# A planned order for the attention stage, its output kept turned, and a mixing stage that loads rows turned

## The reference, cut to what matters

```
z = rms(x, g_pre_mix) @ w_in -> q, k, v, forget logits, B, C, u
s = q.k / 8 + c[query] - c[key], c = cumsum(log_sigmoid(f)), key <= query, 8 heads of 64
o_attn = softmax(s) @ v                     (the sample rows: 512 cached keys and their own 64)
o_conv = B * causal_conv3(C * u)            (512 channels)
merged = concat(rms(o_attn, g_attn_out), rms(o_conv, g_conv_out))
x = x + rms(merged @ w_o, g_post_mix)
x = x + rms(relu(rms(x, g_pre_mlp) @ w_up)^2 @ w_down, g_post_mlp)
```

## Time and profile before

| | us |
|---|---|
| median of three runs | 2732.44 |
| the profiled execution | 2737.44 |
| its span, first to last instruction | 2735.8 |
| PE busy | 2664.9 (97%) |
| DVE busy | 1515.6 (55%) |
| ACT busy | 1126.6 (41%) |
| POOL busy | 1300.7 (48%) |

### The profile page before, as it was taken

The page is one execution under the profiler, slowest core; times in us unless marked ns, Lnnn a source line. Parts: engine busy times, 40 slices in busy tenths (PEclk is TensorE's granted clock), DMA queues, the critical chain, the costliest instruction groups (busy, mean ns, idle before and its releaser), DMA issues.

```text
span 2735.8 us, 41595 instructions
## 1 busy us (share of the span) xinstructions
PE 2664.9 (97%) x14966; PEld 2405.3 (88%) x14966; DVE 1515.6 (55%) x2603; ACT 1126.6 (41%) x2099; POOL 1300.7 (48%) x884
## 2 busy tenths in 40 slices
PE   8999999998999999999999999899999999999997
PEld 8999999897888888888889989889999988999996
DVE  5233344247888887765344344665556564556554
ACT  3201301107777877555333332534333344333433
POOL 3233334220101006553477776766556677566654
PEclk9999999999999999999999999999999999999999
DMA  6643534574565443568444546421211272212213
GB/s 199 199 123 110 175 108 142 189 199 103 124 150 122 100 102 117 167 183 244 143 168 163 196 169 225 170 74 64 77 61 61 85 277 96 73 61 66 72 61 108
DMA packets 294353, 364.26 MB, mean 133 GB/s; under 512 B 37576, under 2 KB 245392, under 8 KB 290128
## 3 DMA queue, kind: packets, MB, share of 16 engines
q1 hardware_dynamic: 257152, 316.15, 37.7%
q0 software_dynamic: 11808, 26.74, 3.1%
q10 hardware_dynamic: 25264, 19.66, 2.1%
HBM read 264.30 MB, written 97.94 MB: 132 GB/s over the span
## 4 chain that ended last, share of the span: by engine, by line
PE 46%; DVE 2%; POOL 1%; DMA 1%; issue 1%; ACT 0%; SPq 0%; DVEq 0%; POOLq 0%; ACTq 0%
PE dn_bank L3006 17%; PE up_bank L2982 15%; PE dn_bank L2962 7%; PE up_bank L2937 7%; DMA m_raw_up<-in_w_up 1%; DVE m_raw_up L2758 1%; POOL m_y L2517 1%; POOL m_w_up L2466 1%; DVE m_t L2758 0%; SPq L2342 0%; ACT m_junk L2659 0%; DVE m_y L2863 0%; DMA m_x<-scratch_x 0%; POOL m_u L2509 0%; DVE m_y L2817 0%
## 5 line engine op out<-in xcount | busy, mean ns | idle before, releaser
L3006 PE MATMUL dn_bank<-m_w_dn,m_u 128*128 128x512 f32 x2304 | 531.0, 391 | 5.4 <-ACT m_y L2692 4.3
L3006 PEld LDWEIGHTS dn_bank<-m_w_dn,m_u 128*128 128x128 f32 x2304 | 432.7, 188 | 96.0 <-ACT m_y L2692 4.0
L2982 PE MATMUL up_bank<-m_h,m_w_up 128*128 128x384 f32 x2688 | 476.1, 337 | 8.7 <-DVE m_stage L2772 4.5
L2982 PEld LDWEIGHTS up_bank<-m_h,m_w_up 128*128 128x128 f32 x2688 | 470.1, 189 | 12.7 <-issue 5.1
L2819 DVE TENSOR_TENSOR m_y<-dn_bank,m_y 128x1024 f32<-128x1024 f32 x168 | 205.7, 1224 | 270.4 <-PE dn_bank L3006 270.4
L508 POOL TENSOR_TENSOR w_lo<-w_raw,w_hi 128x1024 fp32r<-128x1024 f32 x72 | 176.0, 2448 | 342.3 <-DVE w_hi L722 342.3
L2509 POOL TENSOR_TENSOR m_u<-m_stage,m_u 128x384 fp32r<-128x384 f32 x128 | 141.5, 1128 | 281.7 <-ACT m_u L2648 281.7
L2466 POOL TENSOR_TENSOR m_w_up<-m_raw_up,m_w_up 128x512 fp32r<-128x512 f32 x128 | 192.2, 1521 | 65.2 <-ACT m_w_up L2616 65.2
L938 PE MATMUL proj<-ha_hi,w_hi 128*128 128x384 f32 (+1 forms) x640 | 212.1, 331 | 0.0
L1446 DVE TENSOR_TENSOR p_lo<-t_bank,p_hi 128x512 fp32r<-128x512 f32 (+1 forms) x336 | 197.9, 599 | 25.2 <-ACT p_hi L1393 24.6
L938 PE MATMUL proj<-ha_hi,w_lo 128*128 128x384 f32 (+1 forms) x640 | 210.0, 328 | 0.0
(11 more groups left out here) (304 smaller groups left out, 5674.4 us busy)
## 6 DMA issues: line engine op xcount, KB each, us to landing
m_raw_up<-in_w_up SPq DMA_DIRECT2D x48, 1024.0 KB, 5.4
m_raw_dn<-in_w_down SPq DMA_DIRECT2D x47, 1024.0 KB, 4.9
w_raw<-in_w_in SPq DMA_DIRECT2D x72, 512.0 KB, 4.1
scratch_h_pairs<-m_pieces POOLq DMA_DIRECT2D x12, 1792.0 KB, 8.2
m_h<-scratch_h_pairs SPq DMA_DIRECT2D x14, 1536.0 KB, 10.8
nck<-scratch_ncum SPq DMA_DIRECT2D x8, 1312.0 KB, 19.2
scratch_v_hl<-vhl SPq DMA_DIRECT2D x20, 512.0 KB, 2.7
q_hi<-scratch_q_hi SPq DMA_DIRECT2D x16, 528.0 KB, 7.3
```

The costliest lines, as they stand in the source:

```text
L2982: mm = pe.matmul(out, w_up[:, j, wp, k, :], hidden_rows(g, j, hp, k), start=(k == 0 and p == 0), stop=(k == KH - 1 and p == 2))
L3006: mm = pe.matmul(bank[:, cols], part, wd[:, wp, b, cols], start=(b == 0 and p == 0), stop=(b == 1 and p == len(passes) - 1))
```

## The change

**The order.** `attention_order` is written anew: it simulates TensorE, VectorE and ScalarE with a cost for each step and lets each engine take, among the next S, M, T, V and O, the one that can start first (with a fixed preference where several can). The group EXTRA stands behind group 0. There are four s_banks instead of three, and no n_bank.

**The output stays turned.** ScalarE copies the two halves of the o_bank to partitions 0 to 63 (two copies of 64 partitions), GpSimd adds and scales them. The factors lie along columns now, so VectorE's reciprocals are stored to a scratch and loaded back, broadcast to 64 partitions. The result is stored to scratch_attn_t. The next head's loads are spread over the first three groups: queries and keys, decays, values.

**Mixing loads both kinds of rows turned.** No multiplication by g_attn or g_conv per tile: the gains are multiplied into w_o before it is split, one more GpSimd operation per block. GpSimd squares both kinds of rows, sums their blocks and forms both rests; TensorE makes two one-column products per tile and no turns of ag.

The diff, cut to its core (A_BUFS is the number of output buffers; the parts left out rename, drop what is no longer used, or move an operation as told above):

```diff
-S_BANKS, T_BANKS, O_BANKS = 3, 3, 1
-V_BEHIND = 3
-SPLITS = {(1, QT // 4): (4,), (1, 0): (5, 6), (1, 1): (7, 0, 1), (1, 2): (2, 3)}
+S_BANKS, T_BANKS, O_BANKS = 4, 3, 1
 P_BUFS = 4
-A_BUFS = 5
-DELAY = {"act": {"M": 6, "T": 1, "O": 3, "N": 2}, "dve": {"M": 1, "T": 3}}
+A_BUFS = 2
+GROUP_ORDER = (0, EXTRA, 1, 2, 3)
+SPLITS = {0: (5, 6), EXTRA: (4,), 1: (7, 0, 1), 2: (2, 3)}
+FIRST_CHOICE = {"pe": "TVS", "dve": "TS", "act": "OTM"}
...
+    def cost(engine, x):
+        if engine == "pe":
+            if x.kind == "S":
+                return 2 * (x.width / 2.4 + 13) + (107 if x.last else 0), 320
...
+            def store_scales(q):
+                line = dr["rtotal"][q.head:q.head + 1, q.rows]
+                sp.wait_ge(recip_done, q.k + 1)
...
+                    sp.dma_start(line.rearrange("o (a p) -> (o p) a", p=P), rtotal[:, sums(q)], allow_slow_non_contiguous=True).then_inc(rtotal_stored, 16)
+            def load_scales(q):
+                sp.wait_ge(rtotal_stored, 16 * (q.k + 1))
+                if q.k >= 2:
+                    sp.wait_ge(att_done, q.k - 1)
...
+                sp.dma_start(scales[0:HD, q.k % 2, 0:wide(q)], line.to_broadcast([HD, wide(q)])).then_inc(scales_loaded[q.k % 2], 16)
+            def fetch(head, at):
+                par = head % 2
+                if head >= 2 and at == 0:
+                    sp.wait_ge(used, P_BUFS + groups[GROUPS_OF * (head - 1) - 1].products[-1].at + 1)
+                if head == HEADS:
+                    if at == 0:
+                        front.load_weights(sp)
+                elif at == 0:
...
+            for q in groups:
+                fetch(q.head + 1, q.k % GROUPS_OF)
+                store_scales(q)
+                load_scales(q)
...
+                if q.k:
+                    store(groups[q.k - 1])
...
+            def close(q):
...
+                pool.wait_ge(o_taken, O_BANKS + q.k + 1)
...
+                pool.tensor_tensor(place, halves[0], halves[1], ALU.add).then_inc(added, 1)
+                pool.wait_ge(added, q.k + 1)
+                pool.wait_ge(scales_loaded[q.k % 2], 16 * (q.k // 2 + 1))
+                pool.tensor_tensor(place, place, scales[0:HD, q.k % 2, 0:wide(q)], ALU.mult).then_inc(att_done, 1)
+            for q in groups:
+                if q is final[3]:
+                    pool.wait_ge(taken, S_BANKS + ALL_TAKEN)
+                    front.set_ones(pool)
+                    front.sum_blocks(pool, 0, 0)
+                    front.rests(pool, 0, 0)
+                close(q)
+                if q.head == HEADS - 1 and q.g in SPLITS:
+                    for k in SPLITS[q.g]:
+                        front.split_weights(pool, k)
...
+                    act.wait_ge(used, P_BUFS + q.products[-1].at + 1)
+                    if q.k >= 2:
+                        act.wait_ge(added, q.k - 1)
+                    bank = o_bank[q.k % O_BANKS]
+                    act.activation(o_t[0:HD, q.k % 2, 0, 0:q.wide], bank[0:HD, 0:q.wide], ACT.Copy)
+                    act.activation(o_t[0:HD, q.k % 2, 1, 0:q.wide], bank[HD:P, 0:q.wide], ACT.Copy).then_inc(o_taken, 1)
...
     def split_weights(self, pool, k):
         pool.wait_ge(self.w_loaded[k], 16)
+        pool.wait_ge(self.S["gains_loaded"], 32)
+        pool.tensor_scalar(self.w_raw[:, k, :], self.w_raw[:, k, :], self.gains[:, k:k + 1], None, ALU.mult).then_inc(self.S["w_scaled"], 1)
...
+    def sum_blocks(self, pool, t, s):
...
+            pool.tensor_tensor(q[:, n], rows[:, s], rows[:, s], ALU.mult).then_inc(S["squared"], 1)
...
+        pool.tensor_tensor(q[:, :, 0:2, :], q[:, :, 0:2, :], q[:, :, 2:4, :], ALU.add).then_inc(S["halves_summed"], 1)
...
+        pool.tensor_tensor(self.square_sums[:, :, :], q[:, :, 0, :], q[:, :, 1, :], ALU.add).then_inc(S["blocks_summed"], 1)
+    def rests(self, pool, t, s):
...
+        pool.tensor_tensor(self.a_lo[:, s], self.a_in[:, s], self.a_hi[:, s].bitcast(F32), ALU.subtract).then_inc(S["a_lo_done"], 1)
...
+        pool.tensor_tensor(self.c_lo[:, s], self.c_in[:, s], self.c_hi[:, s].bitcast(F32), ALU.subtract).then_inc(S["c_lo_done"], 1)
...
-            last_rows["scores_free"]()
-            turn(0, 0)
+            last_rows["scores_free"](pe)
             pe.wait_ge(S["w_lo_done"], CJ)
             pe.wait_ge(S["c_lo_done"], 1)
             multiply(c_bank, c_hi, c_lo, 0, CJ, S["c_mult"], (0,))
```

More of the change, by code:

```diff
@@ new lines, with __init__ @@
+EXTRA = QT // 4
+GROUP_ORDER = (0, EXTRA, 1, 2, 3)
+SPLITS = {0: (5, 6), EXTRA: (4,), 1: (7, 0, 1), 2: (2, 3)}
+FIRST_CHOICE = {"pe": "TVS", "dve": "TS", "act": "OTM"}
+class Group:
+    def __init__(self, k, head, g):
+        self.k, self.head, self.g, self.par = k, head, g, head % 2
+        self.extra = g == EXTRA
+        self.tiles = [QT] if self.extra else list(range(4 * g, 4 * g + 4))
+        self.n = len(self.tiles)
+        self.rows = slice(SEQ, ROWS) if self.extra else slice(4 * g * P, 4 * g * P + 4 * P)
+        self.wide = P if self.extra else 512
+        self.set = 0 if self.extra else g % 2
+        self.before = None
+        self.scores, self.maxima, self.turns, self.products, self.out = [], [], [], [], None
@@ new lines, in __init__, with attention_steps, step @@
+        self.blocks, self.cols, self.turn = blocks, cols, turn
+        self.first, self.last = first, last
+        self.maximum, self.last_score = None, None
+def attention_steps():
+    groups, count = [], dict.fromkeys("SMTVO", 0)
+    def step(kind, group, **more):
+        count[kind] += 1
+        return Step(kind, group, count[kind] - 1, **more)
+    for head in range(HEADS):
+        for g in GROUP_ORDER:
+            q = Group(len(groups), head, g)
+            same = [p for p in groups if p.set == q.set and not (q.extra and p.head == head)]
+            q.before = same[-1] if same else None
+            for tile in q.tiles:
+                if q.extra:
+                    pieces = [(0, PAST), (PAST, DEC)]
+                else:
+                    pieces = [(c, min(512, (tile + 1) * P - c)) for c in range(0, (tile + 1) * P, 512)]
+                for n, (col, width) in enumerate(pieces):
+                    q.scores.append(step("S", q, tile=tile, n=n, col=col, width=width, last=n == len(pieces) - 1))
+                q.maxima.append(step("M", q, tile=tile, n=len(pieces), width=pieces[-1][0] + pieces[-1][1]))
+                for x in q.scores[-len(pieces):]:
+                    x.maximum = q.maxima[-1]
+                q.maxima[-1].last_score = q.scores[-1]
+            if q.extra:
+                units = [(tuple(range(CB)), slice(0, CB * P)), ((CB,), slice(0, P))]
+            else:
+                units = [((j,), slice(max(0, j - 4 * g) * P, 512)) for j in range(4 * g + 4)]
+            for n, (blocks, cols) in enumerate(units):
+                edge = dict(first=n == 0, last=n == len(units) - 1)
+                t = step("T", q, blocks=blocks, cols=cols, width=cols.stop - cols.start, **edge)
+                q.turns.append(t)
+                q.products.append(step("V", q, blocks=blocks, cols=cols, width=cols.stop - cols.start, turn=t, **edge))
+            q.out = step("O", q, width=q.wide)
+            groups.append(q)
+    return groups
@@ L1335, in _ @@
+            front.load_rows(sp)
+            store(groups[-1])
+            for q in groups[-A_BUFS:]:
+                stored(q)
         @block.gpsimd
         def _(pool):
-            pool.sem_inc(added, 1)
             pool.memset(q_hi[1][:, ROWS:].bitcast(F32), 0.0)
@@ L1406, in _ @@
[L1406 to L1415 removed]
+                    act.wait_ge(turned, 1 + x.at + 1)
+                    act.wait_ge(used, x.at + 1)
@@ L1417, in _ @@
+            for x in queues["act"]:
+                step(x)
         @block.vector
@@ L1502, in step @@
                     mm.then_inc(used, 1)
-                elif x.kind == "N" and not (x is last_n and it == AGAIN):
-                    pe.wait_ge(o_taken, O_BANKS + upto("N", it, x.at) + 1)
-                    pe.wait_ge(n_taken, upto("N", it, x.at) + 1)
-                    for i in range(4 if x.g < EXTRA else 1):
-                        mm = pe.transpose(n_bank[:, i * P:(i + 1) * P], o_t[:, x.at % 2, i * P:(i + 1) * P], ident[:, :])
-                    mm.then_inc(in_rows, 1)
-            loop(pe, "pe", step)
```

657 lines of the change are left out of this document (245 added, 412 removed).

## The result

| | us |
|---|---|
| changed kernel, median of four runs | 2905.42 (2899.59 to 2909.27) |
| kernel before, beside it, median of four | 2731.84 |
| ratio | 1.063, 95% interval 1.0609 to 1.0652 |
| forecast | 2713, range 2698 to 2731 |

The account below looks back on a forecast made before the run. TensorE's stream plus hand-over waits was taken to bound attention, the stream alone mixing. From 2737.44: -31 heads, +13.5 late mixing start, +1.7 clock, -3.7 mixing gave 2718; less 5.0 to the median, 2713 us, range 2698 to 2731.

Parts of the forecast that it names:

- I cost it at nothing in heads 0 to 6: Attention: the reciprocals' store and broadcast load add nothing in the first seven heads, being covered by 10 us.
- (c): Attention: factor round trips on SP pace the heads, deciding from about 5 us a store; 2776 at 7 us; chance 0.08.
- The MLP stage's code is the same; I put nothing there: MLP stage, behind mixing: no change in time, 0 us in the sum.
- I take the cast's 1.04: Last head, GpSimd: each of eight multiplications of w_o by the gains takes 1.04 us.
- W: Last head: issue of the w_o loads, 1028.80 in the kernel before; TensorE forecast to start mixing at W + 69.2.
- Heads: Attention, heads 0 to 6: 57.5 us falls to 53.1, gaining 4.4 each, 31 in all (13 to 40).
- (b): Attention: the new order moves waits instead of removing them, only the turns go; 2731 us, no change; chance 0.12.
- The last head: GpSimd's chain starts mixing 13.5 us later, TensorE idles 17 us, and a lower clock costs 1.7.
- the bound of 2.4: Last head, GpSimd: multiplication by the gains as slow as a two-input operation, 2.4 instead of 1.12 for each of eight, +10.
- (a): Start of mixing is not late: the reciprocals' store overtakes the loads or GpSimd has room; 2703 us; chance 0.14.
- Mixing: Mixing stage: TensorE loses the turns of ag and gains pairs of one-column sums, a gain of 3.7 us.
- (d): Mixing: GpSimd's operations are stretched and bound it, 13.4 us a tile instead of 12.3, +19, 2732 us; chance 0.04.

Follow-up runs that it names:

- e15: Changed kernel with the gains in dead bytes so that no tile is shifted, factor stores as they are: 2865.19 us, ratio 1.0480.
- e13: e1 with the gains in dead bytes so that no tile is shifted, outputs still not divided: 2716.52 us, ratio 0.9941.
- e1: Changed kernel with no reciprocals stored or loaded, scales filled once with 1.0, outputs not divided: 2734.65 us, ratio 1.0002.
- e12: Kernel before with 32 unused bytes added, shifting the tiles that the change shifted: 2758.37 us, ratio 1.0097.
- e14: Changed kernel with factors stored in 16-byte pieces and no tile shifted, gains' multiplications still on GpSimd: 2727.09 us, ratio 0.9979.
- e9: Changed kernel with 16-byte factor pieces, stored and loaded ahead of the next loads, gains multiplied on ScalarE, no tile shifted: 2704.77 us, ratio 0.9879.
- e6: Changed kernel with each stored factor 64 bytes from the next and scales loaded from another tensor, outputs wrongly scaled: 2743.55 us, ratio 1.0040.
- e2: Changed kernel with each 512-factor store writing 16-byte pieces, order in memory changed, outputs wrongly scaled: 2743.42 us, ratio 1.0034.
- e3: Changed kernel with each factor store issued twice, the second into its own scratch, both waited for: 2902.19 us, ratio 1.0622.
- e5: e1 with the gains' tile padded, so later tiles are shifted by 64 bytes instead of 32: 2742.31 us, ratio 1.0035.
- e8: Changed kernel with 16-byte factor pieces, stored and loaded ahead of the next loads, gains multiplied on ScalarE, gains' tile padded: 2729.09 us, ratio 0.9984.

## Why the prediction was wrong

**The step that failed** is "I cost it at nothing in heads 0 to 6". Its cover was worked out from when the factors come, with round trips of the size of the loads. The rival for it, (c), had the right mechanism (a late factor holds GpSimd, GpSimd the copy) and said that SP decides from 5 us a store. It got 0.08, because a load of 512 four-byte elements took 2.4 us. That row was of the wrong direction: the load reads neighbours, the store writes them, and the write took 9.2 us and more. With five stores of 9.5, its sum of 27 us of loads and the stores would give 74.5 us a head, and 75.6 were measured, but this is luck: SP waits 57 us a head for stores, since the first stands behind the loads (21 us), and is not waiting for them in the other 18. Neither the forecast nor the rival has the second path, the next head's decays behind the stores, which is about half of TensorE's idle time (18.0 of 39 us). What the round trips cost the kernel is 148.7 us (e15 less e13) or 170.8 (after less e1).

**The second step that failed:** "The MLP stage's code is the same; I put nothing there". The code is the same, its places in memory are not, and this was to be read in the change. By stages the shift is 3 us in mixing and 14 to 16 behind it (e1 and e13, after and e15); in the kernel before it is 4 and 10 (e12).

**A mis-sized term** is the third: the multiplication of w_o by the gains, "I take the cast's 1.04", took 2.85 us. The fair measure is e14, the whole change with neither unforeseen cost. Its time is 2727.09, 14 above the sum's 2713. Its factors come as forecast (the scaling starts at W + 17.0, forecast 18.3), but mixing starts at W + 82.7, forecast 69.2, and TensorE is idle for 23 us, not 17:

```profile
1083.54 0.77 PE L1929 MATMUL c_bank<-wo_hi,c_hi 128*128 128x512 f32 x1 [23.44 <-POOL c_lo L1658]
```

The same 14.5 us for the eight multiplications make nearly all of it.

**Heads.** Forecast 53.1, measured 53.0, in e13 (outputs not divided) over two heads:

```profile
787.30:893.22 105.92, 105.36 (x665) 90.61 (x665) 96.55 (x299) 89.90 (x173) 21.83 (x20) 1.00 0.51 128
```

TensorE is idle for 0.6 us of 106, against 6.1 of 115. Rival (b) is refuted.

**The last head.** GpSimd's chain sets the start of mixing, as forecast. The gains' multiplication went beyond even the bound of 2.4. In e13, without the factors' wait, the chain begins earlier: W is 999.10 and mixing starts at 1071.37, W + 72.3, forecast 69.2, so two errors nearly cancel. TensorE is idle 16.5 us, forecast 17, and this match is luck too: its last output product ends at W + 55.8 where the forecast had W + 52, so the last head's own gain did not come. Rival (a) is refuted as well: e13 has no factors to wait for and is still late. With the factors in 16-byte pieces (e14) attention is 11 us longer than in e13, and 10 of these lie behind the last head's loads of queries: the wait for the factors behind the w_o loads (9.9 us on GpSimd), which the forecast had in its sum.

**Mixing.** Forecast -3.7; e9, without the idle stretch ahead of it, has 208.2, -3.6. With the idle stretch (e13) it is 210.4, and the granted clock is 0.50 (1.2 GHz) in the 4.2 us behind it, where e9 has 1.00: 2.2 us, forecast 1.7. Rival (d) is refuted: GpSimd is busy for 152.6 of 210.8 us, 9.0 a tile, forecast 8.7.

**The sum.** e13 is the change without its two unforeseen costs, but also without the factors' wait that the sum counts: 2716.52, against 2713. By profiled executions the match is partly luck: -12.9 in attention (forecast -17.5), -1.4 in mixing (-2.0, the clock with it), and -8.4 behind it, in a stage where nothing differs from before, not even the places on the chip. The profiled execution of before was 5 us above its median, and these may lie there: it has a wait of TensorE for ScalarE's m_y of 4.3 us in the MLP (its row above), which e12's and e9's rows don't have. The rest is open. The forecast's own range also has a slip: 5.4 us a head and a scaling of 1.0 give 2705, not 2700.

**The best version** is e9_low, 2704.77 us, 1.2% below the kernel before, with nothing left out: planned order, factors in 16-byte pieces and issued ahead of the next loads, gains on ScalarE, no tile moved.

## What to carry to other kernels

A small transposing store on a queue whose engine waits for it is not small: look for a row of a store, not a load, of that pattern, and where there is none, give the rival the weight of the missing row. Then see what else stands behind the store in the same queue. Here the next head's decays did, and they held TensorE as long as the factors did. Lay a partition's values side by side in memory and let the reader take the stride. When a tile is added, see what it moves: compare the places of the large matmul operands, and put small tiles into dead bytes.

## What the runs showed of the hardware

- 512 four-byte writes to neighbouring places of memory were complete after 8.2 to 11.2 us (quiet stores), though in the one looked at the packets were over in 1.6; 64 bytes apart 1.8 to 3.9 us (e6); in pieces of 16 bytes 1.8 to 3.8 (e2); and two such stores to two tensors together 9.1 to 10.8 (e3). 64 of them took 6.6 us, and 2.1 when apart. That neighbours are written one after another in the memory fits all five, but was not measured; nor was a distance other than 64 bytes.
- Tiles 32 bytes off their places cost 26 us of 2732 (e12), 64 bytes off still more (e5 against e1: 7.7). In the MLP's last products the rows m_u moved, the weights m_w_dn (but for a group's last chunk) did not. The first products have moved weights too, and took no longer: 476.1 us before, 475.2 in e12. Which operand it is, and which multiple would be good, was not tried.
- GpSimd's multiplication of 128x1024 by one number a partition took 2.85 us, more than the subtraction of two tensors of that size (2.35); ScalarE's took 1.16 (e8).
